# All weight casts of a two-layer decoder trunk on ScalarE, in place of a split between ScalarE and VectorE

## The reference

```python
def _layer(x, pos, st, p, lb):
    z = jnp.einsum('btd,dp->btp', x, w_in).astype(f32)
    (q_a, k_a, v_a, o_a, i_a, f_a, q_b, k_b, v_b, g_b,
     q_c, f_c, i_c, g_c, x_d, bg_d, cg_d) = _split_cols(z)
...
    hA, C1, n1, m1 = _mlstm_chunked(...)
    yA = jax.nn.sigmoid(o_a) * _head_rms(hA, norm_a)
...
    hB, Sr1 = _retention_chunked(qb, kb, heads(v_b, H_B), log_gamma, Sr0)
    yB = jax.nn.silu(g_b) * _head_ln(hB, norm_b)
    kc = (1.0 - lbh) * jax.nn.sigmoid(-fc)
...
    hC, Sh1 = _gla_chunked(jax.nn.silu(heads(q_c, H_C)), kc, heads(i_c, H_C), log_f, Sh0)
    yC = jax.nn.silu(g_c) * _head_rms(hC, norm_c)
    yD = bg_d * yconv
    branches = jnp.stack([yA, yB, yC, yD], axis=2)
    proj = jnp.einsum('btnw,nwd->btnd', branches, w_branch)
    gates = jax.nn.sigmoid(jnp.einsum('btd,de->bte', x, w_gate) + b_gate).reshape(bsz, t, N_BRANCH, D_MODEL)
    mix = jnp.einsum('btd,de->bte', jnp.sum(gates * proj, axis=2), w_out)
    h = _layer_norm(ALPHA * x + mix, ln1_g, ln1_b)
    ff = jnp.einsum('btf,fd->btd', jnp.square(jax.nn.relu(jnp.einsum('btd,df->btf', h, w_up))), w_down)
    out = _layer_norm(ALPHA * h + ff, ln2_g, ln2_b)
```

## Time and profile before

| what | us |
|---|---|
| median of 3 runs | 1510.01 (1509.89 to 1512.62) |
| profiled execution | 1510.41 |
| its span, first to last instruction | 1508.6 |
| PE busy | 1491.7 (99%) |
| DVE busy | 949.4 (63%) |
| POOL busy | 943.7 (63%) |
| ACT busy | 679.6 (45%) |
| mean granted TensorE clock | 0.998 |

### The profile page before, as it was taken

How to read it: one execution, slowest core, us unless ns; L and a number is a source line. 1 busy time by engine, 2 the same in 40 slices (tenths; PEclk the granted TensorE clock), 3 DMA queues, 4 the chain that set the end, 5 groups by cost and what they waited for, 6 DMA issues and landing times.

```text
span 1508.6 us, 26528 instructions
## 1 busy us (share of the span) xinstructions
PE 1491.7 (99%) x10373; PEld 1443.3 (96%) x10373; DVE 949.4 (63%) x1909; ACT 679.6 (45%) x1202; POOL 943.7 (63%) x737
## 2 busy tenths in 40 slices
PE   9999999999999999999999999999999999999997
PEld 8999999999999999999999999999999999999997
DVE  4765357668777777744346643667678777777434
ACT  5834444444444544433357344444443445344332
POOL 7766465555556666787767665555555566767873
PEclk9999999999999999999999999999999999999999
DMA  7533554444545454444434336444454444454442
GB/s 262 174 114 122 158 185 131 140 148 142 180 142 169 127 155 153 144 151 152 141 117 140 123 112 191 152 142 141 137 170 151 128 156 149 145 152 143 153 146 86
DMA packets 66548, 223.37 MB, mean 148 GB/s; under 512 B 8056, under 2 KB 12664, under 8 KB 66424
## 3 DMA queue, kind: packets, MB, share of 16 engines
q1 hardware_dynamic: 66424, 221.67, 46.9%
HBM read 206.07 MB, written 15.58 MB: 147 GB/s over the span
## 4 chain that ended last, share of the span: by engine, by line
PE 93%; DVE 3%; DMA 2%; ACT 2%; issue 1%; POOL 0%; SPq 0%; DVEq 0%; ACTq 0%
PE gps L1424 27%; PE gps L1426 27%; PE gps L1425 27%; DMA raw<-in_w 2%; PE xp L1617 1%; PE xp L1676 1%; PE xp L1674 1%; PE xp L1578 1%; PE xp L1588 1%; PE xp L1667 1%; PE xp L1565 0%; PE xp L1596 0%; PE xp L1572 0%; PE xp L1579 0%; PE gps L1565 0%
## 5 line engine op out<-in xcount | busy, mean ns | idle before, releaser
L659 POOL TENSOR_TENSOR low<-raw,whi 128x512 fp32r<-128x512 f32 x724 | 938.0, 1318 | 542.8 <-ACT whi L680 353.4
L1424 PE MATMUL gps<-xh,whi 128*128 128x320 f32 (+1 forms) x2000 | 637.8, 319 | 2.5 <-DVE xl L914 1.6
L1426 PE MATMUL gps<-xh,low 128*128 128x320 f32 (+1 forms) x2000 | 620.8, 310 | 0.0
L1425 PE MATMUL gps<-xl,whi 128*128 128x320 f32 (+1 forms) x2000 | 620.7, 310 | 0.0
L1424 PEld LDWEIGHTS gps<-xh,whi 128*128 128x128 f32 x2000 | 376.9, 188 | 9.9 <-POOL low L659 1.8
L1425 PEld LDWEIGHTS gps<-xl,whi 128*128 128x128 f32 x2000 | 378.6, 189 | 3.2
L680 ACT ACTIVATE whi<-raw 128x1024 fp32r<-128x1024 f32 x272 | 286.6, 1054 | 208.4 <-PE gps L1426 106.6
L1426 PEld LDWEIGHTS gps<-xh,low 128*128 128x128 f32 x2000 | 378.3, 189 | 0.0
L1424 PE MATMUL gps<-ah,whi 128*128 128x320 f32 x640 | 199.4, 312 | 0.2
L1426 PE MATMUL gps<-ah,low 128*128 128x320 f32 x640 | 198.0, 309 | 0.0
L1425 PE MATMUL gps<-al,whi 128*128 128x320 f32 x640 | 198.0, 309 | 0.0
(11 more groups left out here) (328 smaller groups left out, 1824.8 us busy)
## 6 DMA issues: line engine op xcount, KB each, us to landing
raw<-in_w SPq DMA_DIRECT2D x360, 512.0 KB, 3.5
s<-in_st SPq DMA_DIRECT2D x24, 512.0 KB, 4.2
out_ss<-s SPq DMA_DIRECT2D x24, 512.0 KB, 5.0
con<-in_cst SPq DMA_DIRECT2D x4, 462.0 KB, 4.7
out_sp<-pst SPq DMA_DIRECT2D x24, 64.0 KB, 5.0
mix<-in_x SPq DMA_DIRECT2D x4, 320.0 KB, 5.1
out_y<-mix SPq DMA_DIRECT2D x8, 160.0 KB, 1.9
raw<-in_w SPq DMA_DIRECT2D x4, 256.0 KB, 4.9
```

The lines of the kernel that those rows point to most:

```text
L659: nc.gpsimd.tensor_tensor(low_of(c)[:, half, :], raw[:, c % RAWS, half, :], whi[:, c % HIGHS, half, :].bitcast(F32), ALU.subtract).then_in ...
L1424: M(out, hi, xhi, start=start, stop=False)
L1425: M(out, hi, xlo, start=False, stop=False)
L1426: return M(out, lo, xhi, start=False, stop=stop)
```

## The change

`hi_engine` names ACT for every tile. ACT's `split_hi` then does all casts and DVE's returns at once each time; the waits of POOL and PE, which ask `hi_engine` whose counter to look at, follow. The four `whi` buffers stay four.

```diff
 def hi_engine(c):
 
-    behind = SLOTS[(c - HIGHS) % NSLOT]
-    return "dve" if c >= HIGHS and sigmoids(behind) and behind[1] not in ("qC", "gC") else "act"
+    return "act"
```

## The result

The changed kernel takes 1518.67 us (median of 4 runs, 1518.05 to 1520.98), the kernel before 1510.99 in the same comparison (4 runs, 1509.89 to 1512.62). The ratio is 1.0052 with a 95% interval of 1.0038 to 1.0066: slower by 7.7 us, with the whole interval above one. The forecast was 1516.9, the range 1512.5 to 1519.5. Of the 1.8 us between forecast and result, 0.8 is loss (7.7 for 6.9) and 1.0 is the kernel before, whose median is 1510.99 here and was 1510.01 when the forecast was made.

The account below looks back on a forecast made before the run. PE bounds the kernel, so only its waits count: 1.2 + 5.2 + 0.8 - 0.3 = +6.9 us, from the profiled 1510.41 to 1517.3, given as 1516.9 since the runs' median is 0.4 lower; range 1512.5 to 1519.5.

Parts of the forecast that it names:

- What bounds the kernel: PE is busy 1491.7 of 1508.6 us, so only making its stops longer, shorter or new counts.
- The four places: Behind fC 0, oA 2, gate C 5, gB 1, a cast delays ACT's next instruction and PE: 1.2 + 5.2 us.
- my 0.82: Behind oA 2 and gB 1, the cast ahead of `seen` makes PE 0.82 us later each time.
- a_score: At a_score 0, POOL's later halves hold DVE's L1149 0.4 us longer, twice: +0.8, bounds -1.0 and +0.8.
- a_cum: POOL's pair comes later, so DVE's L1126 is let go 0.3 us earlier in one layer: -0.3, bounds -0.8 and 0.
- The other 80 casts I cost at nothing: Casts outside fC 0, oA 2, gate C 5, gB 1: hidden, 0 us; 5.6 if the fins lost their cover.
- the forecast's own case: The sum of the priced terms holds: 1513.4 to 1517.9 us by its bounds, chance 0.72.
- C: More than the sum: landing waits in front of `seen`, or fin B uncovered; +2.4 to +2.8 more, 1519.5; chance 0.10.
- A: Not slower: DVE's relief outweighs, 1508.3 us; num places under 0.2 later; chance 0.08, 0.05 of it for about 1506.
- B: Half is made up: PE, late at a num place, finds its next partner ready; +2.0 us, some 1512; chance 0.10.
- The engines' time: Pricing all 88 casts by ACT's extra 0.332 us each: 29.2 us, or 1539; the forecast did not adopt it.
- time lost at the fins: A sign that the forecast is wrong: the loss appears at the fins, whose casts it took as covered.

Follow-up runs that it names:

- e1: The changed kernel with only the 8 casts behind fC 0, oA 2, gate C 5 and gB 1 back on DVE; 1512.51 us, ratio 1.0011.
- e2: The kernel before with only the 8 casts behind fC 0, oA 2, gate C 5 and gB 1 moved to ACT; 1517.89 us, ratio 1.0048.
- e3: The changed kernel, casts behind fC 0, oA 2, gate C 5, gB 1 one instruction later in ACT's queue; 1512.52 us, ratio 1.0011.
- e4: The changed kernel with the 6 casts behind gate C 3, gate D 2 and gate D 3 back on DVE; 1518.94 us, one run.
- e6: The changed kernel with POOL filling zeros instead of subtracting for the 8 tiles behind gate D 0 to 3; 1519.02 us, one run.

## Why the prediction was right, and where it was not

*What bounds the kernel.* Right: PE's waits alone decided, not the 92 us more work on ACT. e1 and e2 divide the loss into 1.3 for eighty casts and 6.6 for eight, measured apart, which make 7.9 for 7.7.

*The four places.* Right in place and size: forecast 1.2 + 5.2 = 6.4, measured 1.30 + 5.39 = 6.7 by the steps, and e3 shows that the place in ACT's queue is the cause. The num steps came out 0.05 above my 0.82.

*a_score.* Forecast +0.8, measured +0.71 by the mechanism named; DVE's subtraction lasted 1.61 instead of 1.26. The text called the slot gate C 4; the row at 219.74 is gate C 3's, as e4 shows. *a_cum.* Forecast -0.3 in one layer, measured -0.33 there and -0.13 in the other, by the mechanism named: DVE's instruction took 0.31 in the first layer, where it had taken 0.64.

*"The other 80 casts I cost at nothing."* This is the step that failed: it is a term of +1.65 at slot 90. The cover that I checked was ACT's own: at the fins L794 did have room. I had not asked of each of these casts what POOL would do when it came from ACT at another moment. At the fins and in b_rope a pair of POOL's now lies over DVE's two-input instructions: DVE's L1184 went from 546 to 911 ns on average over 24 (the groups of instructions on DVE, before and after):

```profile
L1184 DVE SCALAR_TENSOR_TENSOR hh<-hh,prm,rs 128x320 f32<-128x320 f32 x24 | 13.1, 546 | 0.0
```
```profile
L1183 DVE SCALAR_TENSOR_TENSOR hh<-hh,prm,rs 128x320 f32<-128x320 f32 x24 | 21.9, 911 | 0.0
```

Of the 63.5 us that left DVE, 63.5 - 38.6 = 25 came back as longer DVE instructions, 8.8 of them in this one line. Most of it is hidden; besides a_score it reaches PE at slot 90, +1.65 for both layers. The kernel before had an order there that no line states. Its cast behind gate D 1 ran ahead of the eviction, so that POOL's pair was over (398.63 + 2.54) before the fin began at 401.53. Its casts behind gate D 2 and gate D 3 stood in DVE's queue behind the fin and behind the rope, so that POOL could not begin earlier: the pair of gate D 2 lay over one rope instruction alone (L1162 at 407.58).

*Not priced, the other way.* num C 2 gave back 0.73, since the weight's landing, for which ACT's cast waits there with `seen` behind it, came sooner: in the first layer 4.2 us behind its issue and not 4.8. PE's lateness does not explain that, for SyncE issues the fetch 0.03 behind the end of PE's slot in both kernels. Across the runs the wait follows the landing and not how late PE is: in the changed kernel (PE 0.9 late by then), in e2 (1.7 late) and in e3 (0.4 late) the casts there are

```profile
176.80 1.06 ACT L679 ACTIVATE whi<-raw 128x1024 fp32r<-128x1024 f32 x1 [0.24 <-DMA raw<-in_w]
```
```profile
178.19 1.06 ACT L683 ACTIVATE whi<-raw 128x1024 fp32r<-128x1024 f32 x1 [0.85 <-DMA raw<-in_w]
```
```profile
176.41 1.06 ACT L682 ACTIVATE whi<-raw 128x1024 fp32r<-128x1024 f32 x1 [0.33 <-DMA raw<-in_w]
```

against 0.80 before. Whether the change has a part in the sooner landing stays open. The slots of br B gave 0.33: their cast on DVE had waited for a landing ahead of the eviction, and on ACT it stands behind it (in e2, with that cast on DVE but the landing sooner, the steps are the same). The terms that the prediction had priced come to 6.69 + 0.71 - 0.46 = 6.9, as forecast; the missed loss of 1.65 and the missed gains of 1.06 nearly cancel, so that the sum came close to 7.7 partly by luck. The time of 1518.67 lies above the 1517.9 to which the forecast's own case went, and inside the range by the half of C that was added to it.

*The rivals.* A is excluded by its own sign, since PE falls back by 0.87 to 0.94 at each of the three num places and not by less than 0.2, and DVE's relief brought nothing that reaches PE but the 0.8 at a_cum and br B. B's making up did not come: the four places kept their full price, and the 0.73 above is a landing's. C's landing in front of `seen` is real (num C 2, slot 37 in e2 and e6, slot 85 in e4 and e6), but is not part of this loss. The rule of the Trainium skill, "Perfetto Trace Analysis", section "Optimizing Scalar/DVE Operations", to move work off DVE if DVE is saturated, pointed the right way. The engines' time, priced at 29.2 us in the prediction, is no measure of the loss, since e1 moves 80 of the 88 for 1.3 us. What the Trainium skill, "SBUF — State Buffer", section "Who interferes with whom", says of the lock between DVE and GpSimd agrees with the runs: stretched DVE instructions end just behind one of POOL's, ACT's cast is 1052 ns beside the same POOL, and with short fills in place of the subtraction the stretch is gone (e6). I had cited it as a reason for relief; it was the reason for a loss.

*What would show it.* The wait for `seen` was to grow to about 5 us: it is 5.0, in 7 waits rather than 10. DVE's busy time was to fall by 63: it fell by 38.6. One sign of being wrong, time lost at the fins, came true in part: a stretched fin stands in the chain that costs 1.65 at slot 90, though stretched by POOL and not by a late L794 on ACT.

## What to carry to other kernels

Work moved to an in-order engine costs the delay of what stands behind it there: price the place in the queue, not the duration, and try one place later before another engine. A move also shifts the start of whatever consumes the result: ask of each consumer (here POOL) what it will lie over then. Laying two traces over each other by the ends of PE's slots, and reading the steps of the lag, shows every place at once, to a few hundredths of a microsecond. A step that hangs on a landing has to be looked up in further runs before it is put down to the change: the one at num C 2 in the first layer was -0.53 in the changed kernel, +0.05 in e2 and -0.46 in e3.

## What the runs showed of the hardware

A DVE instruction as small as 4x384 or 128x64 that met POOL's subtraction lasted until a POOL instruction ended: 1.61 and 1.19 us where 0.55 and 0.23 were measured apart from it. Beside POOL's fills, which read nothing, one DVE cast of 128x640 still took 0.80 in place of 0.49; the timeline of e6 has it, and the same line undisturbed:

```profile
401.45 0.99 POOL L659 MEMSET low<- 128x512 f32 x2 [4.22 <-ACT whi L682]
...
401.99 0.80 DVE L1226 CAST yh<-bd 128x640 fp32r<-128x640 f32 x1
...
409.07 0.49 DVE L1226 CAST yh<-bd 128x640 fp32r<-128x640 f32 x1
```

The first ends 0.35 behind the end of the fills, at 402.44. It does so in both layers. And a fetch that lands in time in most runs was late in some, and cost PE up to 1.1 us at one place (slot 85 in e4 and e6, slot 37 in e2 and e6), the size of an effect that one looks for here.
